# Attention outputs copied by VectorE one step earlier; banded attention scores alternate between two pairs of accumulation banks

## The reference, cut to what matters

```
u = rms_norm(x) @ w_in                    # one projection, columns for groups A, B, C, D
A: latent attention, 4 heads, causal      # q = rms_norm(c_q) @ w_uq, kv = rms_norm(c_kv) @ w_ukv, rotary
B: pooling over windows 2, 4, 8, 16, then a linear map
C: banded attention, window 128, 4 heads over 2 kv heads, with a sink per head
D: b_gate * (conv3(c_gate * h) + conv_b)
y = concat of the four, each rms-normalised over its 256 channels
x = x + y @ w_mix_out
```

## Time and profile before

| | us |
|---|---|
| median of 3 executions | 1412.0 (1408.92, 1412.0, 1412.09) |
| profiled execution | 1408.89 |
| its span in the trace | 1407.2 |
| PE busy in the span | 1238.8 (88%) |
| VectorE, ScalarE busy | 703.2 (50%), 356.3 (25%) |
| mean granted TensorE clock | 0.921 of full speed |
| mixer steps, layer 0 | 103.9 (first S) to about 273.6 |
| mixer steps, layer 1 | 796.2 to about 966.6 |

### The profile page before, as it was taken

One profiled execution on the slowest core, in us unless ns is written; L12 is line 12 of the kernel. 1 busy time (PEld: TensorE's weight loads), 2 busy tenths in 40 slices (PEclk: granted clock), 3 DMA queues, 4 the chain that ended last, 5 costly groups with the idle time before them and its releaser, 6 DMA issues.

```text
span 1407.2 us, 17804 instructions
## 1 busy us (share of the span) xinstructions
PE 1238.8 (88%) x5132; PEld 664.3 (47%) x5132; DVE 703.2 (50%) x1677; ACT 356.3 (25%) x745; POOL 68.6 (5%) x125
## 2 busy tenths in 40 slices
PE   5999798998846999999989997899976679999996
PEld 2854455456534344444357544455644444444443
DVE  2335524455566346556553354445556644555554
ACT  3214221114242222222142132220154222222220
POOL 7000000000022200000000000000000100000000
PEclk9999788998968999999999997889988789999999
DMA  8030013081000899999531100221800019999991
GB/s 267 18 120 0 1 43 107 1 343 46 1 0 2 291 407 416 417 421 422 228 130 61 60 1 1 60 91 50 339 1 1 1 41 378 417 420 423 419 408 60
DMA packets 53672, 243.16 MB, mean 173 GB/s; under 512 B 7904, under 2 KB 20480, under 8 KB 28512
## 3 DMA queue, kind: packets, MB, share of 16 engines
q1 hardware_dynamic: 50912, 240.40, 43.1%
q0 software_dynamic: 2688, 1.91, 0.7%
HBM read 240.19 MB, written 2.10 MB: 172 GB/s over the span
## 4 chain that ended last, share of the span: by engine, by line
PE 76%; DVE 12%; issue 5%; ACT 2%; DVEq 2%; ACTq 1%; DMA 0%; POOL 0%; POOLq 0%
PE ps L2309 16%; PE ps L1981 10%; PE ps L2342 8%; PE ps L1973 8%; PE ps L2078 8%; PE ps L2293 5%; PE ps L1952 4%; PE ps L2294 4%; PE ps L2011 3%; PE ps L2238 2%; PE ps L2054 2%; DVE neg_max L1226 1%; PE ps L2279 1%; PE ps L2067 1%; ACT Prx L858 1%
## 5 line engine op out<-in xcount | busy, mean ns | idle before, releaser
L2309 PE MATMUL ps<-wgu,xw 128*64 128x512 f32 x1024 | 228.6, 599 | 18.7 <-ACTq L1105 17.5
L1981 PE MATMUL ps<-hT,ring 128*128 128x512 f32 x352 | 166.4, 630 | 0.0
L1823 DVE TENSOR_TENSOR X<-ps,X 128x512 f32<-128x512 f32 x256 | 156.0, 682 | 12.8 <-issue 10.9
L2309 PEld LDWEIGHTS ps<-wgu,xw 128*64 128x64 f32 x1024 | 75.7, 139 | 166.3 <-issue 166.3
L2342 PE MATMUL ps<-wdn,hhT 128*64 128x512 f32 x512 | 121.2, 617 | 3.3 <-ACTq L1123 3.3
L2293 PE MATMUL ps<-yhi,Wt 128*128 128x512 f32 x256 | 114.1, 446 | 4.6 <-DVEq L1168 3.7
L2078 PE MATMUL ps<-ring,yT 128*128 128x512 f32 x256 | 117.0, 609 | 0.0
L1981 PEld LDWEIGHTS ps<-hT,ring 128*128 128x128 f32 x352 | 70.1, 204 | 84.9 <-issue 84.9
L2294 PE MATMUL ps<-ylo,Wt 128*128 128x512 f32 x256 | 101.0, 395 | 0.0
L1841 DVE SCALAR_TENSOR_TENSOR ylo<-ps,ws,yhi 128x512 fp32r<-128x512 f32 x64 | 48.1, 751 | 75.6 <-ACTq L1133 75.6
L1830 DVE TENSOR_TENSOR hh<-ps,silu 128x256 f32<-128x256 f32 x32 | 13.6, 424 | 133.5 <-ACTq L1111 133.5
(11 more groups left out here) (359 smaller groups left out, 1626.7 us busy)
## 6 DMA issues: line engine op xcount, KB each, us to landing
wgu<-in_w_gate SPq DMA_DIRECT2D x64, 1024.0 KB, 9.0
wgu<-in_w_up SPq DMA_DIRECT2D x64, 1024.0 KB, 11.1
wdn<-in_w_down SPq DMA_DIRECT2D x64, 1024.0 KB, 10.3
ring<-in_w_in SPq DMA_DIRECT2D x8, 1024.0 KB, 6.9
ring<-in_w_mix_out SPq DMA_DIRECT2D x12, 512.0 KB, 5.9
w_kv<-in_xa_w_kv SPq DMA_DIRECT2D x2, 2048.0 KB, 11.9
ring<-in_w_in SPq DMA_DIRECT2D x2, 2048.0 KB, 15.8
ring<-in_w_in SPq DMA_DIRECT2D x2, 1536.0 KB, 16.1
```

Source lines behind the costliest of these rows:

```text
L1823: tt(xh, bank, xh, ALU.add).then_inc(mfreed((what, n)), 1)
L1981: last = mm(bank, w[:, c, c0:c0 + P], hT[:, c, :], start=c == 0, stop=c == KD - 1)
L2309: last = mm(bank[r], xw[:, c, r], wgu[2 * parity + j][:, :, c, :], start=c == 0, stop=c == KD - 1)
```

## The change

Two things. First, in VectorE's `attend` the scaled copy of a finished pair into yT moves from step n-4 to step n-3: into the same step in which PE finishes the pair and ScalarE squares it. It still waits for ScalarE's square. Second, the plan of the banks. The banded scores, which all used banks 0 and 1, use banks 0 and 1 in even steps and 2 and 3 in odd ones. The other jobs of steps 0 to 8, which had banks 2, 3 and 7, now share banks 5 and 7. From step 9 on the banks are as before, but for the counts.

```
-    b.use(("B", 0), 2)
+    b.use(("B", 0), 5)
 
     def between(n):
         if n == 0:
-            b.use(("B", 1), 3)
+            b.use(("B", 1), 7)
         if n == 1:
-            b.use(("qA", 0), 7)
-            b.use(("kvA", 0), 2)
-            b.use(("qA", 1), 3)
+            b.use(("qA", 0), 5)
+            b.use(("kvA", 0), 7)
+            b.use(("qA", 1), 5)
             b.use(("kvA", 1), 7)
         if n == 2:
-            b.use(("qA", 2), 2)
-            b.use(("kvA", 2), 3)
-            b.use(("qA", 3), 7)
-            b.use(("kvA", 3), 2)
+            b.use(("qA", 2), 5)
+            b.use(("kvA", 2), 7)
+            b.use(("qA", 3), 5)
+            b.use(("kvA", 3), 7)
         if n == 3:
-            b.use(("D", 0), 3)
+            b.use(("D", 0), 5)
         if n == 4:
             b.use(("D", 1), 7)
         if n == 5:
-            b.use(("pool", 0), 2, frees=2)
-            b.use(("pool", 1), 3, frees=2)
+            b.use(("pool", 0), 5, frees=2)
+            b.use(("pool", 1), 7, frees=2)
         if n == 6:
-            b.use(("qAT", 0), 7)
-            b.use(("kAT", 0), 2)
-            b.use(("qAT", 1), 3)
+            b.use(("qAT", 0), 5)
+            b.use(("kAT", 0), 7)
+            b.use(("qAT", 1), 5)
             b.use(("kAT", 1), 7)
-            b.use(("stY", 0), 2)
+            b.use(("stY", 0), 5)
         if n == 7:
-            b.use(("qAT", 2), 3)
-            b.use(("kAT", 2), 7)
-            b.use(("D", 2), 2)
+            b.use(("qAT", 2), 7)
+            b.use(("kAT", 2), 5)
+            b.use(("D", 2), 7)
         if n == 8:
-            b.use(("qAT", 3), 3)
+            b.use(("qAT", 3), 5)
             b.use(("kAT", 3), 7)
-            b.use(("stY", 1), 2)
+            b.use(("stY", 1), 5)
...
     if unit[0] == "swa":
-        return 0
+        return 2 * (n % 2)
...
-                    if 4 <= n <= len(list_) + 3 and list_[n - 4][2] == NT - 1 and list_[n - 4][0] != "xa":
-                        kind2, pair2 = list_[n - 4][:2]
+                    if 3 <= n <= len(list_) + 2 and list_[n - 3][2] == NT - 1 and list_[n - 3][0] != "xa":
+                        kind2, pair2 = list_[n - 3][:2]
                         bank = emptied(dve, l, ("O", kind2, pair2))
-                        c = stat_of(list_[n - 4])
+                        c = stat_of(list_[n - 3])
                         ts(yT[:, c], bank, g_out[:, c:c + 1], None, ALU.mult).then_inc(freed(("O", kind2, pair2)), 1)
                         signal("yT_ready")
```

## The result

Before 1410.46 us (median of 4, 1408.7 to 1412.09), after **1391.24** us (1389.49 to 1392.36), on the same chip: ratio 0.9863, 95% interval 0.9843 to 0.9883. The forecast was 1398, with a range of 1389 to 1409. The profiled execution spans 1390.2 us, before 1407.2: 17.0 less. VectorE and ScalarE are as busy as before (704.0 and 356.3), PE is busy 1231.6 against 1238.8 and the mean clock is 0.925 against 0.921, so part of the gain is matmuls that run faster.

What follows compares the result with a forecast made beforehand. The prediction took PE's instruction stream as the bound; its terms summed to -6.1 us per layer, -12.2 for two layers, giving 1396.7 or 1399.8 depending on the base, taken as 1398 us, range 1389 to 1409.

Steps and rivals of the forecast that it cites:

- steps 1, 2: Head projections sharing two banks wait for the copy two jobs before: +1.8 us per layer, bounds +1.3 and +2.6.
- steps 5 to 7: Score wait goes, but other bank and copy waits take up most of it: -0.5 us per layer, bounds -1.5 and +1.5.
- step 8: A sum now in bank 5 waits for ScalarE to empty it: +2.3 us per layer, bounds +2.2 and +3.5.
- D2 and D3: Projections of 16 matmuls each in the mixer; the forecast had no term for a change in their duration.
- step 11: Value sum's 4.7 us wait for its bank goes, with the slow projection behind it: -6.6 us per layer.
- step 15: Value sum's 3.31 us wait goes, until the next transposes wait for ScalarE's copy: -3.7 us per layer.
- register instructions: More of them before waits on VectorE and ScalarE, some six on the chain: +0.6 us per layer, bounds 0 and +1.5.
- rival of new slow stretches: Enlarged gap in step 2 and new one in step 8 each cost 1.9 us more: some 1405; chance 0.18.
- A slow D2: Sign of being wrong: this mixer projection, 8.63 us before, runs slow after the change.
- part 2: New bank plan of steps 0 to 8: per layer +1.8, -0.5, +2.3, and +0.6 us for register instructions.
- more is won: Rival: steps 5 to 7, head projection, registers and step 15 come out better, -8.2 per layer, some 1393; chance 0.17.
- the slower case: Rival: low clock holds through D2 and D3, adding 5.0 and 6.5 us, +5.4 per layer, some 1421; chance 0.09.

Runs made afterwards that it cites:

- Experiment 6: Second kernel of experiment 4 with one step 8 sum put behind a just-filled bank: 1364.76 us; or with the yT copy one step late again: 1387.09 us.
- experiment 3: Changed kernel with the head projections of steps 1 and 2 rotating over three banks instead of two: 1387.22 us.
- experiment 5: The changed kernel run once more, unaltered: 1391.61 us.
- experiment 2: Changed kernel with one sum of step 8 moved from bank 5 to the free bank 2: 1389.49 us.
- yT-only kernel: Kernel before with only VectorE's yT copy moved one step earlier, banks as they were: 1385.97 us.
- experiment 4: yT-only kernel with the last head projection in idle bank 5: 1369.13 us; then also two step 6 jobs moved, to banks 5 and 1: 1360.4 us.
- banks-only kernel: Changed kernel without the earlier yT copy, so only the bank table and alternating score banks against the kernel before: 1413.15 us.

## Why the prediction was right, and where it wasn't

| per layer, us | forecast | layer 0 | what was measured |
|---|---|---|---|
| steps 1, 2 | +1.8 | -1.9 | start of S(5) after the first S |
| steps 5 to 7 | -0.5 | +0.8 | start of D2, from S(5) |
| step 8 | +2.3 | +2.5 | start of S(9), from S(8) |
| D2 and D3 | 0 | +1.5 | duration of each, 16 matmuls |
| step 11 | -6.6 | -6.9 | start of S(12), from S(11) |
| step 15 | -3.7 | -3.6 | start of O(13), from S(15) |
| register instructions | +0.6 | not seen | |
| mixer | -6.1 | -7.7 | start of the last O |

In layer 1 the same rows are -1.9, -0.5, +2.2, +1.1, -6.7 and -3.5, and the mixer -8.0; the rest, +1.4, lies in steps 12 to 14, where O(10) and S(13) ran slower than before.

- **Steps 11 and 15** carried the sum and held: gap and slow stretch went together, nothing was late behind D5, and T(14)'s second half was late behind ScalarE's copy. Experiment 6 puts the waits back: step 11 is 7.3 us longer in both layers, step 15 2.9 and 3.7.
- **Steps 1 and 2 are the mis-sized term**, by 3.7 us per layer and with the wrong sign. The walk through the waits was right: qA(1), then qA(3) wait for the copy two jobs before, and 1.1 us more idle time came. What failed is "nearer the lower end since the slow stretch there is present before too": I took the slow stretch as present in both kernels. It costs 3.1 us (experiment 3) and was not there after: 1.1 more idle time less 3.1 gives -2.0, and -1.9 was measured. Experiment 3 moves the gaps back and has it again; experiment 5 shows that its absence repeats. My rival of new slow stretches expected one more at this place, where one went.
- **Steps 5 to 7.** The gain of S(6) was indeed swallowed by the wait for bank 4. Waiting for VectorE's pool copy in step 6 (up to 1.4) wasn't in the walk. In layer 1 the same steps came out at -0.5, since there the kernel before had waited 3.86 for ScalarE's qTA copy where layer 0 had waited 2.68, and VectorE's pool copy cost 0.68 after.
- **Step 8.** The wait is 2.04 us in both layers, as walked, and the term was met. D2 and D3 around it ran slower, 1.5 in layer 0 (9.35 for 8.63 and 8.44 for 7.70), for which only the rivals had a price. A slow D2 was one of my own signs of being wrong, and it came, though far from the 13.6 of the rival that feared it. With the wait taken out (experiment 2) or put in (experiment 6), S(8) to S(9) moved by 1.9 to 3.1 us in each of the four layers, as the term says. The totals of both layers moved by only 1.8 and 4.4, the first mixed with what happened in steps 1 and 2, the second within the scatter of the runs.
- **Register instructions** (+0.6): no run shows this term, and I found no such sum in the trace. What experiment 2 suggests is another effect: they shift the timing by tenths and thereby where the clock falls.
- **The change as a whole** was forecast as a sum of two halves. The runs say more: VectorE's copy is all of the gain, and the bank table is a loss of 5 us beside it. My part 2 had that sign, and too much of it: +4.2 per layer, although its -0.5 for steps 5 to 7 already held what the copy gives in step 7. I took the bank counts of the diff as they were and didn't ask which of the eight banks was unused. The Trainium skill ("Perfetto Trace Analysis", Matmul Optimizations) advises to see that all 8 PSUM banks are in use. The runs agree in part: the first job put into the idle bank brought 17 us, but the change also puts bank 5 to use and loses by it, since there the other jobs of steps 0 to 8 share two banks instead of three.
- **The range** held partly by luck: of the errors per layer in layer 0, -3.7 in steps 1 and 2 and -0.6 for the register instructions were set off by +1.3 in steps 5 to 7 and +1.5 in D2 and D3. The outcome lies in its lower eighth, close to "more is won" (1393), yet for a reason which that rival didn't name. (Two slips in the rivals' sums, neither of which changes the forecast: "more is won" with step 15 at its best is -8.5 per layer, not -8.2, and D3 took 7.70 before, so the slower case is +5.9 for it, not +6.5.)

What stays open is why two gaps of 1.46 and 1.70 leave the clock up while 0.17 and 1.71 bring it down. The layers counted below show it, but give no rule, and no kernel was run that varies one gap alone.

## What to carry to other kernels

List, for every job that waits for a buffer, which job had it before and which buffers nobody holds at that time; here, giving the waiting job an idle bank was worth 17 us, and rotating the busy ones a loss. An evacuation that hands a buffer back should stand in the step in which its last writer ends, not one later. And when PE is the bound, price a gap with the slow matmuls behind it, but do not carry that second price from one place to another: it has to be measured, and an edit elsewhere can bring it back.

## What the runs showed of the hardware

- The clock's fall doesn't follow the length of the last gap. Gaps of 1.46 and then 1.70 us were followed by full speed in six layers of six; 0.17 and 1.71 (1.67 in layer 1) by a slow stretch in two of two; 1.21 and 2.06 or 2.01 in two of two, in one of them only up to the middle of S(3); a single one of 2.00 to 2.05 in four of four (the kernel before and the yT-only kernel).
- The first matmuls behind a gap can still run at the full clock: 1.12 and 0.74 in experiment 3, and only the next S takes 1.22 instead of 0.70. Before, behind the gap of 2.05, the first pair is slower already (1.48 for 1.02). So slow matmuls can stand some way behind the gap that goes with them. The Trainium skill ("TensorE: Matmul & The Clock Gate", HAM oscillation — how this bites in real kernels) describes a kernel whose PE fell to the lower clock at each of its waits for DMA, of about 3 to 5 us. The traces here agree for the gaps of 4.7 us (D5 at 9.00 and 9.36) and of 3.3 (four mix matmuls at 3.40 instead of 1.98). The gaps of 2.05 are shorter than those waits and were followed by slow matmuls all the same.
- The two kernels of experiment 4 spread by 6 and 9 us from run to run, the banks-only kernel by 6, the changed kernel and the yT-only kernel by less than 3. The kernel of experiment 6 with one more wait spreads by 1.5. Nothing here explains that.
